# An encoder layer on one core: gate buffers, norm positions and update order at the last sub-layer

## What is computed

```python
x = x + 0.5 * rmsnorm(swiglu(rmsnorm(x, gains[0]), w_ffn1_gu, w_ffn1_down), gains[1])
...                                                    # the mixer: recurrence, pooling, gates, w_out
x = x + rmsnorm(m @ w_out, gains[3])
x = x + 0.5 * rmsnorm(swiglu(rmsnorm(x, gains[4]), w_ffn2_gu, w_ffn2_down), gains[5])
e = p.astype(x.dtype) @ w_ple_proj                     # p has 256 features
gate = jax.nn.sigmoid(rmsnorm(x, gains[6]) @ w_ple_gate)
x = x + rmsnorm(gate * e, gains[7])                    # the last sub-layer
```

## Time and profile before

| | |
|---|---|
| median of 3 runs | 2460.96 us (2459.55 to 2463.96) |
| the profiled execution | 2456.82 us, span 2455.0 us |
| mean granted TensorE clock | 0.982 |
| PE busy | 2338.3 us, 95% of the span |
| DVE, ACT, POOL busy | 54%, 47%, 46% |

### The profile page before, as it was taken

How to read it: one execution, slowest core, us unless ns; L and a number is a source line. 1 busy time by engine, 2 the same in 40 slices (tenths; PEclk the granted TensorE clock), 3 DMA queues, 4 the chain that set the end, 5 groups by cost and what they waited for, 6 DMA issues and landing times.

```text
span 2455.0 us, 54105 instructions
## 1 busy us (share of the span) xinstructions
PE 2338.3 (95%) x20814; PEld 2003.4 (82%) x20814; DVE 1329.7 (54%) x2273; ACT 1148.3 (47%) x2085; POOL 1120.7 (46%) x881
## 2 busy tenths in 40 slices
PE   7899999999997999999979999988999999999887
PEld 5788888888886888888758888877888888888776
DVE  7666666500189777778952332387555654000835
ACT  6333333333455666666544333654334333333554
POOL 2677777422213555555535443314777775222110
PEclk9999999999998999999989999999999999999999
DMA  3111111322130111111111122321112112322102
GB/s 128 43 56 53 54 51 51 107 76 70 48 102 19 38 46 46 40 42 47 38 31 52 60 60 77 120 79 33 53 51 60 57 55 87 96 69 66 48 18 72
DMA packets 98519, 147.26 MB, mean 60 GB/s; under 512 B 10480, under 2 KB 43504, under 8 KB 98416
## 3 DMA queue, kind: packets, MB, share of 16 engines
q1 hardware_dynamic: 70352, 121.14, 16.5%
q10 hardware_dynamic: 28064, 24.69, 3.1%
HBM read 131.70 MB, written 14.09 MB: 59 GB/s over the span
## 4 chain that ended last, share of the span: by engine, by line
PE 73%; DVE 12%; issue 6%; POOL 5%; ACT 3%; DMA 1%; DVEq 0%; POOLq 0%; ACTq 0%; SPq 0%
PE bank L848 12%; PE bank L851 12%; PE bank L850 12%; PE bank L817 11%; PE bank L818 11%; PE bank L819 11%; POOL ring L731 3%; DVE work L1944 2%; DVE hid L1946 2%; POOL ring L735 1%; DVE hid L1773 1%; PE bank L974 1%; DMA ring<-weights 1%; ACT ring L1147 1%; DVE ops L1781 1%
## 5 line engine op out<-in xcount | busy, mean ns | idle before, releaser
L848 PE MATMUL bank<-ops,ring 128*128 128x264 f16 x3584 | 995.5, 278 | 32.9 <-DVE work L1908 16.7
L850 PE MATMUL bank<-ops,ring 128*128 128x264 f16 x3584 | 994.8, 278 | 0.0
L851 PE MATMUL bank<-ops,ring 128*128 128x264 f16 x3584 | 994.5, 277 | 0.0
L731 POOL TENSOR_TENSOR ring<-ring 128x512 f16<-128x512 f32 x384 | 496.4, 1311 | 279.7 <-ACT ring L1161 279.7
L817 PE MATMUL bank<-hid,ring 128*128 128x264 f16 x2124 | 587.4, 277 | 1.9 <-DVE hid L2402 1.9
L818 PE MATMUL bank<-hid,ring 128*128 128x264 f16 x2124 | 587.2, 276 | 0.0
L819 PE MATMUL bank<-hid,ring 128*128 128x264 f16 x2124 | 586.9, 276 | 0.0
L718 POOL TENSOR_TENSOR ring<-wtmp,ring 128x512 f16<-128x512 f32 x173 | 205.1, 1189 | 673.5 <-ACT ring L1108 672.3
L848 PEld LDWEIGHTS bank<-ops,ring 128*128 128x128 f16 x3584 | 353.5, 99 | 99.1 <-issue 24.2
L1161 ACT ACTIVATE ring<-ring 128x512 f16<-128x512 f32 x384 | 226.5, 622 | 407.6 <-POOL ring L735 406.0
L851 PEld LDWEIGHTS bank<-ops,ring 128*128 128x128 f16 x3584 | 352.6, 98 | 54.6
(11 more groups left out here) (179 smaller groups left out, 2850.6 us busy)
## 6 DMA issues: line engine op xcount, KB each, us to landing
ring<-weights SPq DMA_DIRECT2D x429, 256.0 KB, 2.7
hid<-xT SPq DMA_DIRECT2D x8, 528.0 KB, 8.3
hid<-out_x ACTq DMA_DIRECT2D x8, 528.0 KB, 7.7
out_x<-hid ACTq DMA_DIRECT2D x8, 528.0 KB, 4.1
ops<-xT ACTq DMA_DIRECT2D x6, 528.0 KB, 7.2
out_x<-ops ACTq DMA_DIRECT2D x6, 528.0 KB, 4.2
ops<-out_x ACTq DMA_DIRECT2D x6, 528.0 KB, 6.5
out_x<-ops SPq DMA_DIRECT2D x12, 264.0 KB, 2.2
```

The source lines that it names most:

```text
L731: nc.gpsimd.tensor_tensor(low(slot), weight_source(name, k), high(slot), ALU.subtract)\
L848: nc.tensor.matmul(out, whi, xhi, start=(kk == 0 and fresh(name, k)), stop=False, skip_group_check=True)
L850: nc.tensor.matmul(out, whi, xlo, start=False, stop=False, skip_group_check=True)
L851: mm = nc.tensor.matmul(out, wlo, xhi, start=False, stop=end, skip_group_check=True)
```

## The change

- gate_buf has four buffers, not two, and the wait of a gate is for the square of tile n-4.
- After the first and second FFN (q = 0 and 2) weight units 5 and up are prepared behind the last tile (position 7) instead of position 6; for q = 2 only units 5 to 7 there, and units 8 and 9 come one each behind the squares of tiles 0 and 1.
- On DVE, for q = 0 and 2, the adds of the next quarter's squares stand ahead of the square sum.
- On ScalarE, q = 2 and g = 3: gate, square and weight for tiles 0 and 1 stand ahead of post norm 25; tile 2 and gate 3 ahead of squares(3, 3), square 3 behind them; tiles 4 and 5 behind h_high(3, 2). gates_and_squares goes on from tile 6.
- On DVE, q = 2 and g = 3: products 0 and 1 and their adds ahead of the update of quarter 3; that update in two parts, each with a product and an add (2, then 3) behind it; product 4 behind the split of quarter 2, product 5 behind split_p(2), the square sum last.
- The hooks of norms 25 to 27 in ple0 and of 28 to 30 in ple1 are at other positions.
- In gated_products the update of quarter g-1 is done in four parts, one between product and add of each of the tiles m = 4 to 7 of quarter g; the last quarter's update follows as a whole.
- The ln table is loaded between gate and square of a quarter's last tile, not behind its gain.

```diff
--- before.py
+++ after.py
@@ -159,6 +159,7 @@
 AHEAD = [0, 3, 0]
 
 SQUARE_PARTS = 2
+GATE_BUFS = 4
 UPDATE_PARTS = [2, 2, 2, 4]
 
 
@@ -488,7 +489,7 @@
             return u1[:, g * N:(g + 1) * N]
 
         def gate_buf(n):
-            return hidv[:, 16 + n % 2, 3, :]
+            return hidv[:, 16 + n % GATE_BUFS, 3, :]
 
         def arr(n):
             return area[:, n * TP:(n + 1) * TP]
@@ -1063,8 +1064,8 @@
                 if i == 0 and t == 1 and k == 0:
                     pe.wait_ge(p_ready, g + 1)
 
-            turn("ple0", 0, "G", ple_rhs, ple_ready, {(0, 6): calls(25), (2, 4): calls(26), (8, 3): calls(27)})
-            turn("ple1", 0, "G", ple_rhs, None, {(10, 2): calls(28), (18, 2): calls(29), (26, 2): calls(30)})
+            turn("ple0", 0, "G", ple_rhs, ple_ready, {(2, 4): calls(25), (4, 0): calls(26), (16, 2): calls(27)})
+            turn("ple1", 0, "G", ple_rhs, None, {(8, 6): calls(28), (16, 6): calls(29), (24, 6): calls(30)})
             norm(31)
 
 
@@ -1273,7 +1274,7 @@
                     next_name = "head0" if q == 0 else "ple0"
                     after[end, 0, 0] = [(next_name, 0, (0, 1))]
                     after[end, 0, 2] = [(next_name, 0, (2, 3, 4))]
-                    after[end, 0, 6] = [(next_name, 0, (5, 6, 7) if q == 0 else (5, 6, 7, 8, 9))]
+                    after[end, 0, 7] = [(next_name, 0, (5, 6, 7))]
 
                 def evac(tiles):
                     for tile in tiles:
@@ -1294,13 +1295,23 @@
                 squares(q + 1, 0)
                 evac(last[1][AHEAD[q]:])
                 for g in range(1, G):
+                    if q == 2 and g == G - 1:
+
+                        gates_and_squares((0,))
+                        prep(next_name, 0, 8)
+                        gates_and_squares((1,))
+                        prep(next_name, 0, 9)
+                        ln_exp_tables()
                     post_norm(g)
                     pre_norm(g - 1)
                     after_g = last[g + 1] if g < G - 1 else []
                     evac(after_g[:AHEAD[q]])
+                    if q == 2 and g == G - 1:
+                        gates_and_squares((2,))
+                        gate_sigmoids((3,))
                     squares(q + 1, g)
                     if q == 2 and g == G - 1:
-                        gate_sigmoids((0, 1))
+                        gated_squares((3,))
                     h_high(q + 1, g - 1)
                     evac(after_g[AHEAD[q]:])
                 if q == 0:
@@ -1309,7 +1320,7 @@
                     silus(1, (0, 1))
                     scale(UPS[1][1], 0)
                 else:
-                    gated_squares((0, 1))
+                    gates_and_squares((4, 5))
                 ln_exp_tables()
                 pre_norm(G - 1)
                 h_high(q + 1, G - 1)
@@ -1630,8 +1641,8 @@
                 for n in ns:
                     name, i, pos, m, g = y_tiles(3)[n]
                     ba, uses_a = plan.job(name, i, pos - 1)
-                    if n >= 2:
-                        _, _, _, m2, g2 = y_tiles(3)[n - 2]
+                    if n >= GATE_BUFS:
+                        _, _, _, m2, g2 = y_tiles(3)[n - GATE_BUFS]
                         act.wait_ge(ysq_added, y_adds(3, m2, g2))
                     act.wait_ge(bank_full[ba], uses_a + 1)
                     nc.scalar.activation(gate_buf(n), bank[ba][:, 0:N], ACT.Sigmoid, scale=1.0 / WS)\
@@ -1649,13 +1660,14 @@
                     if n >= 2:
                         y_gain(n)
                     if m == KD - 1:
-                        ln_exp_tables()
                         norm(CALLS.index(("post", 3, g)))
 
             def gates_and_squares(ns):
 
                 for n in ns:
                     gate_sigmoids((n,))
+                    if y_tiles(3)[n][3] == KD - 1:
+                        ln_exp_tables()
                     gated_squares((n,))
 
             squares(0, 0)
@@ -1724,7 +1736,7 @@
             down(1)
             up(1)
             down(2)
-            gates_and_squares(range(2, KD * G // 2 - 6))
+            gates_and_squares(range(6, KD * G // 2 - 6))
             prep("ple1", 0, 0, 1, 2, 3, 4, 5)
             gates_and_squares(range(KD * G // 2 - 6, KD * G // 2))
             prep("ple1", 0, 6, 7, 8, 9)
@@ -1798,13 +1810,13 @@
                         dve.wait_ge(ysq_added, n)
                     V_.tensor_tensor(ssq(g), ssq(g), pair_buf[:, n % 2, :], ALU.add).then_inc(ysq_added, 1)
 
-            def post(q, g, y):
+            def post(q, g, y, parts=None):
 
                 c = CALLS.index(("post", q, g))
                 dve.wait_ge(rinv_ready, c + 1)
                 if q < 3:
                     dve.wait_ge(x_back[g], backs(q, g))
-                for ks in parts_of(UPDATE_PARTS[q]):
+                for ks in parts_of(UPDATE_PARTS[q])[parts or slice(None)]:
                     step(V_.tensor_tensor(y[:, ks, :], y[:, ks, :], rinv(c).unsqueeze(1).to_broadcast(
                         [P, KD // UPDATE_PARTS[q], N]), ALU.mult))
                     x = xk(min(q + 1, 3), g, ks.start, ks.stop)
@@ -1825,10 +1837,22 @@
                 square_sum(q + 1, 0)
                 add(last[1][AHEAD[q]:])
                 for g in range(1, G):
-                    post(q, g, yq(q, g))
+                    if q == 2 and g == G - 1:
+                        for n in range(2):
+                            gated_product(n)
+                            gated_add(n)
+                        for n in range(2):
+                            post(q, g, yq(q, g), slice(n, n + 1))
+                            gated_product(n + 2)
+                            gated_add(n + 2)
+                    else:
+                        post(q, g, yq(q, g))
                     after_g = last[g + 1] if g < G - 1 else []
                     add(after_g[:AHEAD[q]])
                     h_split(q + 1, g - 1)
+                    if q == 2 and g == G - 1:
+                        gated_product(4)
+                        gated_add(4)
                     if q == 2:
                         split_p(g - 1)
                     if g == G - 1:
@@ -1837,9 +1861,13 @@
                         elif q == 1:
                             products(1, (0, 1))
                         else:
-                            gated_products((0, 1))
-                    square_sum(q + 1, g)
+                            gated_product(5)
+                            gated_add(5)
+                    if q == 1:
+                        square_sum(q + 1, g)
                     add(after_g[AHEAD[q]:])
+                    if q != 1:
+                        square_sum(q + 1, g)
                 h_split(q + 1, G - 1)
                 if q == 1:
                     products(1, (2, 3))
@@ -2391,25 +2419,35 @@
             head_turn(HEADS, True, True)
             gates()
 
+            def gated_product(n):
+
+                name, i, pos, m, g = y_tiles(3)[n]
+                ba, uses_a = plan.job(name, i, pos - 1)
+                b, uses = plan.job(name, i, pos)
+                dve.wait_ge(bank_read[ba], uses_a + 1)
+                dve.wait_ge(bank_full[b], uses + 1)
+                V_.scalar_tensor_tensor(out=hidv[:, Y0 + m, g, :], in0=bank[b][:, 0:N],
+                                        scalar=1.0 / WS, in1=gate_buf(n),
+                                        op0=ALU.mult, op1=ALU.mult).then_inc(bank_read[b], 1)
+
+            def gated_add(n):
+                *_, m, g = y_tiles(3)[n]
+                add_square(3, m, g)
+
             def gated_products(ns):
 
                 for n in ns:
-                    name, i, pos, m, g = y_tiles(3)[n]
-                    ba, uses_a = plan.job(name, i, pos - 1)
-                    b, uses = plan.job(name, i, pos)
-                    dve.wait_ge(bank_read[ba], uses_a + 1)
-                    dve.wait_ge(bank_full[b], uses + 1)
-                    V_.scalar_tensor_tensor(out=hidv[:, Y0 + m, g, :], in0=bank[b][:, 0:N],
-                                            scalar=1.0 / WS, in1=gate_buf(n),
-                                            op0=ALU.mult, op1=ALU.mult).then_inc(bank_read[b], 1)
-                    add_square(3, m, g)
-                    if m == KD - 1:
-                        post(3, g, hidv[:, Y0:Y0 + KD, g, :])
+                    gated_product(n)
+                    *_, m, g = y_tiles(3)[n]
+                    if m >= KD // 2 and g:
+                        post(3, g - 1, hidv[:, Y0:Y0 + KD, g - 1, :], slice(m - KD // 2, m - KD // 2 + 1))
+                    gated_add(n)
+                post(3, G - 1, hidv[:, Y0:Y0 + KD, G - 1, :])
 
             down(1)
             up(1)
             down(2)
-            gated_products(range(2, KD * G))
+            gated_products(range(6, KD * G))
 
 
 # ---- launch: the inputs laid out for the chip, feature-major, weights as a stream of tiles ----
```

## The result

| | before | after |
|---|---|---|
| median of 6 runs each | 2460.57 us (2459.05 to 2463.96) | 2446.21 us (2444.91 to 2452.66) |
| ratio | | 0.994, 95% interval 0.9927 to 0.9953 |
| the profiled execution, span | 2456.82, 2455.0 us | 2445.24, 2443.4 us |

The change makes the kernel 14.8 us faster by the ratio (11.6 to 18.0 by its interval), 14.4 by the medians; 10.3 was forecast. The sign and the places are right, two of the three sizes are not. And the two profiled executions differ in more places than the change touches: both FFN loops changed, by 6.7 and 9.0 us in opposite directions, in code that the diff leaves alone. The spans of the two lie 11.6 us apart, near the forecast, only because the loops took back 2.3 us on balance: that is chance.

A forecast was written before the change was run, and what follows sets the result against it. TensorE was taken as busy throughout except at two seams after the FFNs and the tail; gains of 2.0 + 6.7 + 1.6 = 10.3 us take 2460.96 to 2450.7 us, range 2446.0 to 2457.0.

The forecast's parts named there:

- First seam: After the first FFN: adds ahead of the square sum start DVE's update 0.8 us earlier; everything moves by 2.0 us.
- my upper bound: First seam: at most 2.9 us gained, the whole wait before norm 9; the lower bound was 0.
- TensorE's part of the last seam: After the second FFN: the 0.71 and 6.16 us waits go; TensorE runs at full clock through position 13.
- The chain of ScalarE and DVE: Last seam: their queued steps make position 14 wait 1.95 us, norm 27 3.35, and position 18 until 2353.4.
- product 4, its add: Last seam, DVE's steps before the split of p: product 0.45 us, then an add of 0.95 us.
- The size of the last seam: Between second FFN and last sub-layer: 6.7 us gained, the 0.71 included; bounds 1.5 and 10.5.
- The low clock: Last seam: half speed after the 6.16 and 4.63 us idle times costs about 1.4 and 2.1 us.
- rival 4: Last seam: hand-overs are cheaper or the clock stays up, 3.5 us more gain, 2447.2; chance 0.15.
- The tail: Behind the last matmul: 2.3 us instead of 3.46 before norm 31, table loaded meanwhile; 1.6 us gained, bounds 0.5 and 2.5.
- The rule on table loads: Last seam: rows give 1.28 us per load; the skill page adds about 1.38 of drain, a result near 2453.4.
- rival 2: Last seam: a table load between dependent steps costs twice its row, 2.6 us more for two, 2453.3; chance 0.05.
- Rival 5: Last seam: gates and weights ahead of norm 25 delay the update and gate 6; slower, 2468.7; chance 0.05.

The follow-up runs named there:

- e1: The kernel before with the tail's part of the change alone; ratio 1.0002 (0.9984 to 1.002).
- e2: The kernel before with the last seam's part of the change alone; ratio 0.9966 (0.9944 to 0.9987).
- e3: The kernel before with the first seam's part of the change alone; ratio 0.9986 (0.9967 to 1.0005).
- e4: The changed kernel with gate 4 ahead of quarter 2's high parts, gates 6 and 7 ahead of the last ln table, norm 27 at (18,0); ratio 0.9952.
- e7: The kernel before with the new order of POOL's steps in the FFN loops that e6 has; median 2449.38 us, ratio 0.9971.
- e5: e4 with gate 8 ahead of squares 6 and 7 and the next stage's weights 0 to 5 spread behind tiles 9 to 14; 2436.40 us, ratio 0.9913.
- e6: The changed kernel with POOL's steps reordered in the FFN loops' weight pairs (sum 3 ahead of low 2, sum 4 ahead of low 4); ratio 0.9911.
- e8: e5 with e6's order of steps on POOL; 2432.33 us, ratio 0.9901 (0.9877 to 0.9925).
- e9: e6 with two gate buffers instead of four; 2435.41 us.
- e12: The changed kernel with ScalarE making high part 4 of an FFN pair behind both silus, not between them; 2449.06 us, ratio 0.9973.
- e10: e6 with norms 25 and 26 ahead of the first gates again on ScalarE and DVE, norm 26 at (2,6); 2432.56 us.
- e11: e8 with e10's order of norms and gates; 2431.72 us, ratio 0.99 (0.9868 to 0.9931).

## Why the prediction was right or wrong

- **What bounds, and where.** Right: only the two seams and the tail gave anything by the change itself.
- **First seam.** Too low. The step that failed is ScalarE's arrival at the norm "near 717.3", with DVE's gain of 0.8. I took the 1.06 us wait for POOL over from the row, where POOL's low part took 2.07 us behind the start of the square sum; in the new order it takes 1.16 us, the wait shrinks to 0.15, and the update starts 1.9 us earlier, not 0.8 (the rows above). Norm 11 then waits for nothing, and the whole 2.93, my upper bound, is gained. Between the two first profiles 2.0 us are left at norm 12, which is the forecast's number by luck, since the head loop happened to take 1.0 more. What is left there scatters: on one chip 915.8 and 913.4 without the part against 912.6 and 913.0 with it (e1, e2; e3, e4), on another 915.55 (e7, with its low clock) against 909.5 to 910.6 (e5, e6, e8): 0.4 to 6 us.
- **TensorE's part of the last seam**: right to 0.2 us relative to norm 23; no wait and full clock until position 14, which waits 1.50 us, not 1.95 (ScalarE was 0.5 us earlier than the prediction had it).
- **The chain of ScalarE and DVE**: right in order and in its three waits, too long by 1.9 us in all. The step that failed is "product 4, its add": tile 4 is m = 0, whose square starts the sum, so add_square does nothing and DVE goes on to the split of p 0.34 us after the product's start (2337.38 to 2337.72 above): 0.9 us. The trace of before had it to be read: behind its products 0 and 1 DVE makes one add, at 2336.37, not two. Second, norm 27 waited 2.21 us, not 3.35, and ran at full clock: 1.65 to DVE, not 2.18: 0.5 us.
- **The size of the last seam.** Against the profile that I predicted from it gives 8.8 us, not 6.7, and the chain's 1.9 us are nearly all of that: the low clock behind position 18 lasted 3.4 us and not 4.3, but norms 28 to 31 follow one another in 14.04 to 14.14 us and not in 13.94.
- **The low clock.** What other executions give beyond that is a term that I mis-sized on the side of before: I took 1.4 us for the one behind norm 25's wait. In e1, with the same 6.16 us of idle time, the clock stayed at half until about 2327.1, 4.7 us long, not 2.9:

```profile
2322.00:2324.00 2.00, 1.56 (x5) 0.50 0.00 0
2324.00:2326.00 2.00, 2.00 (x11) 0.50 0.00 0
2326.00:2328.00 2.00, 2.00 (x15) 0.72 0.00 0
```

  Norm 20 to the last matmul takes 173.7 us in the profile that I predicted from and 174.6 to 175.4 in the three others with the old seam (e1, e3, e7); with the new one (after, e2, e6, e9, e12) it takes 164.6 to 166.1. Against the changed kernel's own 165.0 the seam gives 8.8 to 10.5 us, not 6.7: 2.1 to 3.8 more, about what rival 4 gave (3.5), on which I had put 0.15. (e1's 175.4 has about 0.5 us of the tail's norms in it.)
- **The tail**: right, 1.17 + 0.43 us.
- **The rule on table loads.** In the seam of after, the sigmoid starts 1.29 us after the load's start (2315.22 to 2316.51). No further drain is in these rows, as in those of before; the Trainium skill (ScalarE: Activation LUTs, section "What ACT_TABLE_LOAD costs"), which puts some 1.38 us of drain on top of the load, is not borne out here, and rival 2 with it. e10 has one load fewer than the change, four for five, where its expectation said two.
- **Rival 5**, slower by gates ahead of norm 25: gates first do cost something, 3.3 us (e10), but no step of the chain came later than worked out, and 15 us were never near.
- **The sum.** 3.0 + 8.8 to 10.5 + 1.6 makes 13.4 to 15.1 us; measured are 14.4 by the medians and 13.2 (14.4 by the means) with the loops cleared of their waits. Forecast were 2.0 + 6.7 + 1.6: the first two terms are the mis-sized ones. Not seen at all was that the loops have two phases, which makes a single profiled execution a poor base: mine had the first loop late and the second free, that of after the reverse. What brings a loop into one phase or the other at its start stays open.

## What to carry to other kernels

Before an operation is priced by a row, check whether the code issues it for that tile; the first tile of a sum often has no add. Cut two profiles at landmarks of the code and compare the segments, those that the change leaves alone too: what differs there is scatter of the kernel, and it can be as large as the gain. Where an engine is put ahead of another by moving work, look at what stands behind the moved work on the third one: gates ahead of a norm bought no time here, since TensorE did not need them yet.

## What the runs showed of the hardware

**Two phases of a loop.** The FFN loops here have 18.9 us of TensorE work a pair and, beside it, a ring of POOL, ScalarE and weight transfer that is nearly as long. Such a loop runs free (18.90 us in every pair) or late (mostly 19.2 to 19.5). Late pairs begin at the loop's start or up to nine pairs on, and then go on to its end. It costs 5 to 9 us a loop and is found in either loop of kernels whose loops are the same code; with the other order on POOL every pair but those at a loop's ends takes 18.90 us in the six profiles that have it (e6 to e11), and with a longer ring both loops are late (e12). That the ring's length decides is argued from these two. What goes with the late phase is more busy time of DVE and POOL for the same work. Ten pairs of the first and the second loop, before and then after (the columns are those of the earlier trace rows):

```profile
200.00:394.00 194.00, 190.68 (x1682) 163.54 (x1680) 123.82 (x201) 73.35 (x130) 140.65 (x111) 1.00 0.18 54
1800.00:1989.00 189.00, 189.00 (x1683) 164.38 (x1681) 110.71 (x200) 73.36 (x130) 136.43 (x111) 1.00 0.19 55
```
```profile
200.00:389.00 189.00, 189.00 (x1683) 164.38 (x1681) 105.64 (x201) 75.56 (x131) 131.88 (x111) 1.00 0.20 56
1800.00:1994.00 194.00, 191.40 (x1688) 164.16 (x1687) 123.87 (x201) 74.00 (x132) 141.08 (x112) 1.00 0.19 55
```

No single instruction marks the phase. DVE's product of two work tiles takes 1.64 us in a late pair of before (217.91) and 0.70 in a free pair of after (217.62), where POOL stands still for most of it; but it takes 1.66 us also in the free second loop of before, and 0.70 and 0.9 to 1.1 in the late second loop of after.

**The clock behind an idle time.** Behind the same idle time TensorE's clock was at half for different lengths of work: behind 6.16 us for 2.9 us (before) and 4.7 (e1); behind 3.05 us for none (e8), 3.1 (e5) and 5.9 (e11). Between e8 and e11 that alone is 2.9 us (an estimate, half of 5.9).
